# One-core hybrid decoder step: second half-batch woven by dependency strands, tanh forms, gates by tokens, value rows placed by load

## The chip, the cores and the metric

The kernel is one program on one NeuronCore of a Trainium2 chip. Its measure is device time in microseconds of that core, from launch to the last instruction. The core's engines run their own instruction streams in program order and meet only at semaphores: TensorE (PE, with its weight load PEld), VectorE (DVE), ScalarE (ACT), GpSimd (POOL) and SyncE (SP). Here POOL only issues gathers of expert rows and SP issues all other transfers.

## The reference, cut to what matters

512 prompt tokens (after 16 meta tokens) and 8 sample tokens go through one layer with D = 1024.

```python
z, xbc, dt_raw, q, k, v, g, g_lr, merge = split(rmsnorm(x) @ w_in)
xbc_c = silu(conv4(xbc)); y = ssd_chunked(...)              # 32 heads in 4 groups, chunks of 128
y_ssd = (rms((y + d_skip * xh) * silu(z)) * ssd_norm_w) @ w_ssd_out     # rms over a group of 512
o = gla_chunked(q, k, v, logsigmoid(g_lr @ up + b) / 16)    # 4 heads, chunks of 64
y_gla = (rms(o) * gla_norm_w * silu(g)) @ w_gla_out         # rms over a head's 256
x = x + (sigmoid(m0) * y_ssd + sigmoid(m1) * y_gla) @ w_out
hn = rmsnorm(x, norm2_w)
# PEER: 8 heads; top 16 of 128 x 128 keys; each chosen expert is a row (u, v) of 2 x 1024 numbers
x = x + sum_{h,k} softmax_gate * gelu(u[idx] . hn) * v[idx]
```

Everything is fp32.

## The kernel before, in words

Three stages (norm, SSD and GLA of the first 256 prompt tokens with the samples) fill the first 480 us or so. The change touches only `stage_tail`, and there it touches the planner and the task bodies.

**Two halves and a PEER loop.** The tail holds half p = 0 (256 prompt tokens and 8 samples, 264 columns: gates z and g, merge gates, output projection, second norm, queries and key scores) and half p = 1 (the other 256 prompt tokens: also SSD and GLA of these tokens, then the same). Weights come in units of 512 KB (`load`, `wring`, a ring of `WR = 4`), one unit feeding 16 PE instructions of 256 columns or 8 of 512. Half 1 has 128 units: 24 of the SSD projection (`su`), 16 of GLA (`gu`), 24 of z and g (`zu`), 40 of merge (`mg`, `my`, `mo`), 8 of output (`ou`), 16 of queries (`qu`).

**PEER units and pairs.** `UNITS` are 33 blocks of 16 expert slots: five rounds `ROUNDS` (token tiles 0, 1, the samples, tiles 2, 3); a tile has 8 units, one for each head, the samples have one. A unit has 8 pairs, 264 pairs in all. A slot is one gather (`ga`, L1684) of 128 rows of 8 KB into a ring of `RING = 10` buffers; `dot` (L2117, DVE) multiplies the u half with hn and sums, `gelu` (L1874, ACT), `gg` (L2124, DVE) multiplies with the gate, then the v half is added either on PE (`diag` L1887 on ACT, then `sum` L2467, four PE instructions of 512 columns into the ACC banks) or on DVE (`acc`, L2136). That last step frees the buffer, and POOL then issues the gather that takes its place. `ch` parts 0 to 3 (DVE) choose the experts of unit u + 2. The split between PE and DVE is fixed: in rounds 0 and 1, from the second head on, slots 0, 2, 3, 4, 6, 8, 10, 11, 12, 14 of 16 go to DVE, all others to PE.

**The order.** `tail_order` writes one list of tasks; each engine executes its own tasks of that list in that order. `peer_order` gives for each pair: dot (both slots), gelu, then `sum` and the new gathers of the pair before, choice, a stretch of half-1 work (`front` 0), gg, diag, acc of this pair, another stretch (`front` 1). The half-1 work is one fixed sequence (`ssd_second`, `gla_second`, `front_half`), cut into stretches by PE cost so that the key scores of half 1 for the second head are done at pair 120 and the rest by pair 160. A wait of one task in that sequence holds all later tasks of its engine, the PEER tasks among them.

**Half 1's gates.** z and g are computed by channels; each slab of y is transposed (`tr`), multiplied by the gate (`mul`), squared (`sq`), summed by `ss` (a PE column of ones), rooted, spread again by `bc` (PE) and applied by `scale` (DVE). silu and sigmoid are ACT functions (L1720, L1792, L1824), each of which loads an ACT table when gelu was the last function, and gelu loads its own back. The GLA state is a chain of four `go` (PE) and `gst` (DVE) steps for each head.

At the end of a round `wfl` loads norm_f over hn_cur, `fadd`, `fsq`, `fms`, `frt`, `fin` finish the tile on DVE and ACT, and SP stores it (`st`), waits for that store (`xl`) and loads the next tile.

Of the kernel before, what the change touches and what calls it, by code (L numbers as in the profile page):

```python
# [997 lines left out]
VECTOR_SLOTS = (0, 2, 3, 4, 6, 8, 10, 11, 12, 14)  # L998
VECTOR_UNITS = [u for u, (r, h) in enumerate(UNITS) if r < 2 and h >= 1]
SLOT_ENGINE = ["vector" if u in VECTOR_UNITS and s in VECTOR_SLOTS else "tensor" for u in range(len(UNITS)) for s in range(TOPK)]  # L1000
SLOT_TURN = [SLOT_ENGINE[:n].count(SLOT_ENGINE[n]) for n in range(len(SLOT_ENGINE))]
# [22 lines left out]
def ssd_second(units, put, use):  # L1024

    def project(g, r, u):
        units.add(("su", g, r, u), False)
        use("su", g, r, u)

    def convolve(g, r):  # L1030
        for kind in ("cvt", "tap", "slu"):
            for j in (2 * r, 2 * r + 1):
                put(0, kind, g, j)

    put(0, "stl", 0)
    for r in range(3):
        project(0, r, 0)
        project(0, r, 1)
        convolve(0, r)
    for g in range(GROUPS):  # L1040
        ahead = [(r, u) for r in range(3) for u in range(2)] if g + 1 < GROUPS else []

        def next_unit():
            if ahead:
                r, u = ahead.pop(0)
                project(g + 1, r, u)
                return [r] if u else []
            return []

        if g + 1 < GROUPS:  # L1050
            put(0, "stl", g + 1)
        for c in range(2):
            put(1.0, "xt", g, c)
            put(.5, "bt", g, c)
            put(1.25, "seg", g, c, 0)
            put(1.25, "seg", g, c, 1)
            put(0, "btc", g, c)
            put(0, "xd", g, c)
            for half in range(2):
                put(0, "dec", g, c, half)  # L1060
                put(0, "mxm", g, c, half)
            done = next_unit()
            put(.9, "yo", g, c)
            put(.9, "cs", g, c)
            put(0, "yof", g, c)
            for r in done:
                convolve(g + 1, r)
            done = next_unit()
            put(2.0, "yd", g, c)
            put(0, "upd", g, c)  # L1070
            put(0, "ys", g, c)
# [7 lines left out]
def gla_second(units, put, use):

    def project(h, u):
        units.add(("gu", h, u), False)
        use("gu", h, u)

    put(0, "gz")
    put(3.4, "glr")
    put(0, "glc")
    for h in range(2):
        put(0, "gsl", h)
    project(0, 0)  # L1090
    put(1.7, "gkp")
    for kind in ("gkb", "gke", "gkn", "gkd"):
        put(0, kind)
    for u in range(1, 4):
        project(0, u)
    for h in range(GH):
        nxt = lambda u: project(h + 1, u) if h + 1 < GH else None
        put(0, "qkv", h)
        put(.5, "cum", h)
        for kind in ("bnd", "gex", "qke"):  # L1100
            put(0, kind, h)
        put(1.0, "kta", h)
        put(0, "ktc", h)
        put(0, "atm", h)
        for j in range(4):
            put(1.1, "go", h, j)
            nxt(j)
            put(0, "gst", h, j)
            if j % 2:
                put(0, "goc", h, j // 2)  # L1110
        put(0, "gss", h)
        if h + 2 < GH:
            put(0, "gsl", h + 2)
        if h % 2:
            put(0, "gos", h // 2)


def front_half(p, units, seq):

    put = lambda cost, *task: seq.append((cost, task))  # L1120
    cost_of = {"zu": 3.6, "mg": 3.6, "my": 3.6, "mo": 3.6, "ou": 3.5, "qu": 3.6, "su": 3.5, "gu": 3.5}
    use = lambda *task: put(cost_of[task[0]], *task)

    put(0, "xload", p)
    if p == 1:
        ssd_second(units, put, use)
        gla_second(units, put, use)
    for s in range(6):
        for u in range(4):
            units.add(("zu", p, s, u), p == 0)  # L1130
    for j in range(KD):
        for i in range(2):
            units.add(("mg", p, j, i), p == 0)
        for u in range(2):
            units.add(("my", p, j, u), False)
        units.add(("mo", p, j), False)
# [7 lines left out]
    if p == 0:  # L1144
        put(0, "ysload", 0)
    put(0, "yload", p, 1)
    for q in range(4 if p == 0 else 0):
        put(0, "xcast", q)
        put(0, "xsub", q)
    for s in range(7):  # L1150
        t = s - 1
        for u in range(4):
            if s < 6:
                use("zu", p, s, u)
            elif u < 2:
                use("mg", p, 0, u)
            else:
                use("my", p, 0, u - 2)
            if t < 0:
                continue  # L1160
            if u >= 1:
                put(.2, "ss", p, t, u - 1)
            if s < 6 and u == 3:
                for a in range(3):
                    put(0, "silu", p, s, a)
            put(.7, "tr", p, t, u)
            for kind in (("mul", "sq") if t < 4 else ("sq", "mul")):
# [1475 lines left out]
```

## Time and profile before

| what | value |
|---|---|
| median of 3 runs | 2611.31 us (2610.52 to 3598.17) |
| profiled execution, its own time | 2614.99 us |
| its span, first to last instruction | 2612.9 us |
| PE / DVE / ACT / POOL busy over the span | 82% / 60% / 28% / 27% |
| mean granted PE clock | 0.904 of full |
| DMA | 751.20 MB, of which the expert rows (queue q0) 545.29 MB |
| first dot starts, last dot ends | 852.3 us, 2598.1 us |

The span is read in three parts: up to the first dot at 852 us (the first stages and half 0); from there to 1905 us, in which units 0 to 15 of PEER are woven with nearly all of half 1; and the rest, units 16 to 32, with the last query units in it. The highest of the three times lies far from the two others and from the profiled one; the median is the figure to compare with.

### The profile page before, as it was taken

What the parts mean: (1) busy time and instruction counts of PE and PEld (TensorE: products, weight loads), DVE (VectorE), ACT (ScalarE), POOL (GpSimd) and SP (SyncE); (2) the same over time, 40 slices, a digit from 0 to 9 for tenths busy, and PEclk for the clock granted to TensorE, in tenths of its full rate; (3) what the DMA queues carried; (4) which work ended last, traced back from release to release, by engine and by line L of the source; (5) the groups of instructions that cost most, each with busy time, mean ns of one, the idle gap of its engine ahead of it and who ended that gap; (6) DMA issues with size and microseconds to landing.
All of it is one profiled execution on the core that took longest, in us unless ns stands there. A gap on an engine that the chain in (4) does not pass through costs nothing.

```text
span 2612.9 us, 24483 instructions
## 1 busy us (share of the span) xinstructions
PE 2130.9 (82%) x7972; PEld 1348.2 (52%) x7988; DVE 1577.6 (60%) x3578; ACT 739.6 (28%) x1761; POOL 702.5 (27%) x636
## 2 busy tenths in 40 slices
PE   5888798699996967776788888997779877787786
PEld 5655365488964645553565666773525433333332
DVE  2556323233213539896666577887866777777764
ACT  2333111232102225443322333222223222222221
POOL 0212122000000222221233232333324444444452
PEclk8999799798998988888898998998879999989899
DMA  5143222442544978886788897999989999999997
GB/s 206 78 157 147 89 99 77 158 146 87 159 157 148 392 281 302 300 301 221 290 312 342 326 388 289 422 424 425 407 243 414 427 427 427 427 427 427 427 426 296
DMA packets 146402, 751.20 MB, mean 288 GB/s; under 512 B 20025, under 2 KB 39033, under 8 KB 77538
## 3 DMA queue, kind: packets, MB, share of 16 engines
q0 software_dynamic: 75008, 545.29, 52.3%
q1 hardware_dynamic: 71266, 204.33, 21.7%
q8 instruction: 64, 1.05, 0.2%
q14 instruction: 64, 0.52, 0.1%
HBM read 718.43 MB, written 31.07 MB: 287 GB/s over the span
## 4 chain that ended last, share of the span: by engine, by line
PE 41%; DVE 18%; DMA 14%; issue 4%; ACT 4%; POOL 1%; SPq 0%; DVEq 0%; POOLq 0%; ACTq 0%
PE bank L2467 12%; DMA t_rows<-in_experts,t_idx 12%; PE bank L2174 10%; PE bank L2404 6%; DVE t_rows L2117 6%; PE bank L2416 3%; DVE t_fin L2136 2%; PE bank L2176 2%; PE bank L2177 2%; PE bank L2178 2%; POOL t_rows L1684 1%; DMA t_hn_cur<-in_norm_f 1%; PE bank L2372 1%; DVE t_junk L1940 1%; DVE t_junk L1936 1%
## 5 line engine op out<-in xcount | busy, mean ns | idle before, releaser
L1684 POOL DMA_INDIRECT t_rows<-in_experts,t_idx x528 | 616.0, 1167 | 1511.9 <-PE bank L2467 662.9
L2467 PE MATMUL bank<-t_rows,t_diag 128*128 128x512 f32 (+1 forms) x1552 | 769.4, 642 | 194.6 <-ACT t_diag L1887 194.2
L2117 DVE CUSTOM_DVE_ANT_0 t_rows<-t_rows,t_hn_cur 128x1024 f32<-128x1024 f32 (+1 forms) x528 | 634.1, 1223 | 167.6 <-DMA t_rows<-in_experts,t_idx 167.3
L2467 PEld LDWEIGHTS bank<-t_rows,t_diag 128*128 128x128 f32 (+1 forms) x1552 | 296.7, 200 | 594.9 <-issue 335.8
L2174 PE MATMUL bank<-t_xs,t_wring 128*128 128x256 f32 (+1 forms) x1664 | 408.9, 403 | 46.6 <-ACT t_last L1712 23.2
L2174 PEld LDWEIGHTS bank<-t_xs,t_wring 128*128 128x128 f32 x1664 | 332.7, 203 | 133.3 <-issue 80.1
L1874 ACT ACTIVATE t_gel<-t_hid 128x2 f32<-128x2 f32 (+1 forms) x264 | 53.7, 203 | 638.2 <-DVE t_hid L2117 638.0
L1887 ACT ACTIVATE t_diag<-ident,t_gg 128x128 f32<-128x128 f32 x372 | 133.5, 395 | 189.5 <-DVE t_gg L2124 188.9
L2136 DVE SCALAR_TENSOR_TENSOR t_fin<-t_rows,t_gg,t_fin 128x1024 f32<-128x1024 f32 x140 | 179.9, 1285 | 7.8
L2404 PE MATMUL bank<-t_yoT,t_wring 128*128 128x264 f32 (+1 forms) x768 | 175.2, 386 | 4.2 <-DVE t_yoT L2076 4.2
L2404 PEld LDWEIGHTS bank<-t_yoT,t_wring 128*128 128x128 f32 x768 | 146.3, 192 | 34.2 <-issue 12.7
L1874 ACT ACT_TABLE_LOAD x78 | 100.1, 1283 | 73.4 <-DVE t_hid L2117 72.3
L2176 PE MATMUL bank<-t_xhl,t_whl 128*128 128x264 f32 x320 | 97.2, 304 | 23.5 <-DVE t_xhl L1962 22.9
L1958 DVE TENSOR_TENSOR t_whl<-t_wring,t_whl 128x1024 fp32r<-128x1024 f32 x40 | 48.9, 1223 | 78.8 <-ACT t_whl L1696 78.8
L418 PE MATMUL bank<-xnT,ring 128*128 128x280 f32 x368 | 94.4, 418 | 1.5 <-PEq L2487 1.5
L2177 PE MATMUL bank<-t_xhl,t_whl 128*128 128x264 f32 x320 | 93.3, 292 | 0.0
L2178 PE MATMUL bank<-t_xhl,t_whl 128*128 128x264 f32 x320 | 93.3, 291 | 0.0
L2124 DVE TENSOR_TENSOR t_gg<-t_gel,t_gates 128x2 f32<-128x2 f32 (+1 forms) x264 | 40.9, 155 | 81.4 <-ACT t_gel L1874 79.6
L418 PEld LDWEIGHTS bank<-xnT,ring 128*128 128x128 f32 x368 | 72.9, 200 | 20.4 <-issue 2.2
L2416 PE MATMUL bank<-t_wring,t_mixed 128*128 128x512 f32 (+1 forms) x160 | 73.6, 610 | 7.5 <-issue 7.5
L2057 DVE TENSOR_TENSOR t_yoT<-bank,t_mixed 128x264 f32<-128x264 f32 (+1 forms) x48 | 20.5, 428 | 94.2 <-PE bank L2354 39.3
L2176 PEld LDWEIGHTS bank<-t_xhl,t_whl 128*128 128x128 f32 x320 | 62.8, 196 | 24.9 <-issue 24.2
(388 smaller groups left out, 2436.0 us busy)
## 6 DMA issues: line engine op xcount, KB each, us to landing
t_wring<-in_w_merge SPq DMA_DIRECT2D x80, 512.0 KB, 4.8
t_wring<-in_w_z SPq DMA_DIRECT2D x32, 512.0 KB, 5.8
t_wring<-in_w_query SPq DMA_DIRECT2D x32, 512.0 KB, 7.9
ring<-in_w_ssd SPq DMA_DIRECT2D x4, 3072.0 KB, 13.2
t_wring<-in_w_ssd SPq DMA_DIRECT2D x24, 512.0 KB, 6.5
t_rows<-in_experts,t_idx POOLq DMA_INDIRECT x528, 14.3
s_sst<-in_state_ssd SPq DMA_DIRECT2D x4, 2048.0 KB, 9.3
o_sssd<-s_sst SPq DMA_DIRECT2D x16, 512.0 KB, 2.6
```

Of the source, the lines that this page charges most:

```text
L418: last = nc.tensor.matmul(ps[MAIN[n % 3]][:, 0:ACOLS], w[:, kt, i * P:(i + 1) * P], k.xnT[:, kt, 0:ACOLS], start=kt == 0, stop=kt == KD - 1)
L1684: nc.gpsimd.indirect_dma_start(rows[0:m, n % RING, :], None, k.dram["experts"], bass.IndirectOffsetOnAxis(idx[0:m, u, s:s + 1], 0)).then_i ...
L1874: nc.scalar.activation(gel[0:m, 2 * g:2 * g + 2], hid[0:m, 2 * g:2 * g + 2], ACT.Gelu).then_inc(gelu_done, 1)
L2117: last = nc.vector.tensor_tensor_reduce(out=v, in0=v, in1=hn_cur[0:m, r % 2, :], scale=1.0, scalar=0.0, op0=ALU.mult, op1=ALU.add, accum_o ...
L2136: nc.vector.scalar_tensor_tensor(fin[:, :], rows[:, n % RING, D:ROW], gg[:, s:s + 1], fin[:, :], ALU.mult, ALU.add).then_inc(acc_done, 1)
L2174: return nc.tensor.matmul(out, wring[:, n % WR, cols], x[:, kt, 0:w], start=first, stop=final)
L2176: nc.tensor.matmul(out, hi, xhl[:, 0, kt, 0:w], start=first, stop=False)
L2177: nc.tensor.matmul(out, lo, xhl[:, 0, kt, 0:w], start=False, stop=False)
L2178: return nc.tensor.matmul(out, hi, xhl[:, 1, kt, 0:w], start=False, stop=final)
L2404: last = nc.tensor.matmul(ps[bank][:, 0:width(p)], wring[:, n % WR, kt * P:(kt + 1) * P], yoT[:, at_k + kt, 0:width(p)], start=kt == 0 and ...
L2416: last = nc.tensor.matmul(ps[2 + 3 * i + c][0:part_rows(c), :], mixT[:, kt, part_cols(c)], wring[:, n % WR, kk * 512:(kk + 1) * 512], star ...
L2467: last = nc.tensor.matmul(ps[bank][0:round_rows(r), :], diag[0:m, d % DIAGS, 0:round_rows(r)], rows[0:m, n % RING, D + half * 512:D + half ...
```

## The change

1. **Strands.** The fixed sequence of half 1 is replaced by some 45 strands, each a list of steps with the tasks that they must follow. A "place" is half a pair (`front` 0 or 1). At each place every strand is asked in turn for steps whose predecessors were emitted at least 1 place before (2 for a step that begins on PE); PE cost is paced so that half 1 ends at place 228 (pair 114), and no place takes more than about 6 us of it. Half 0's rest is taken in gulps of 5 us a place.
2. **Pair order.** dot is one task per slot; gg, diag and acc of the pair before stand between the two dots, `sum` of the pair before follows on PE, then the place, the choice, the second place.
3. **tanh forms.** silu and sigmoid of half 1 (sigmoid of half 0 as well) become ACT Tanh and a DVE `scalar_tensor_tensor`; conv weights are halved once, and the output projection's result is multiplied by .5.
4. **Gates by tokens.** z and g of half 1 are computed by tokens (`zt`), gated and squared there, and one PE product with a diagonal of reciprocal roots (`dg`, `tq`) transposes and scales at once; `ss`, `bc`, `rc`, `scale` go for half 1.
5. **GLA.** Its units are split into `gq` and `gv`; the four chunk products come first (`csp`), one DVE task forms the four states, one PE task the outputs.
6. **Rows by load.** `slot_engines` puts each slot on PE or DVE, whichever has less planned work at that pair.

```diff
-VECTOR_SLOTS = (0, 2, 3, 4, 6, 8, 10, 11, 12, 14)
-VECTOR_UNITS = [u for u, (r, h) in enumerate(UNITS) if r < 2 and h >= 1]
...
+    strand(*[step([("sil", g, CT - 1), of("ups", prev(chunks, i))], 1.5, ("xt", g, c), ("bt", g, c)) for i, (g, c) in enumerate(chunks)])
+    strand(*[step([("bt", g, c), of("yd", prev(chunks, i)), of("mxm", prev(chunks, i), 1)], 0, ("btc", g, c), ("xd", g, c)) for i, (g, c) in enumerate(chunks)])
+    strand(*[step([of("upd", prev(chunks, i)) or ("gkd",), of("dec", prev(chunks, i), 1)], 2.5, ("seg", g, c, 0), ("seg", g, c, 1)) for i, (g, c) in enumerate(chunks)])
+    strand(*[step([("seg", g, c, 1), of("yd", prev(chunks, i))], 0, ("dec", g, c, 0), ("dec", g, c, 1)) for i, (g, c) in enumerate(chunks)])
+    strand(*[step([("xd", g, c), of("ups", prev(chunks, i)), ("stl", g)], 1.8, ("yo", g, c), ("cs", g, c)) for i, (g, c) in enumerate(chunks)])
+    strand(*[step([("dec", g, c, 1), ("btc", g, c)], 0, ("mxm", g, c, 0), ("mxm", g, c, 1)) for g, c in chunks])
+    strand(*[step([("mxm", g, c, 1), ("xd", g, c), of("upd", prev(chunks, i))], 2., ("yd", g, c)) for i, (g, c) in enumerate(chunks)])
+    strand(*[step([("yd", g, c), ("yof", g, c)], 0, ("upd", g, c), ("ys", g, c), *([("sts", g)] if c else [])) for g, c in chunks])
...
     for u in range(len(UNITS)):
         for g in range(PAIRS):
-            order.append(("dot", u, g))
+            order.append(("dot", u, g, 0))
+            if prev is not None:
+                weigh_pair(*prev)
+            order.append(("dot", u, g, 1))
             order.append(("gelu", u, g))
             if prev is not None:
                 finish_pair(*prev)
+            order.append(("front", u, g, 0))
             if g in parts and u + 2 < len(UNITS):
                 choice_part(u + 2, parts[g])
-            order.append(("front", u, g, 0))
-            order.append(("gg", u, g))
-            order.append(("diag", u, g))
-            order.append(("acc", u, g))
             order.append(("front", u, g, 1))
...
+TENSOR_LAG, OTHER_LAG = 2, 1
+PLACE_COST = 6.
+LAST_PLACE = 2 * 114
+ROW_COST = {"tensor": 1.94, "vector": 1.29}
+PAIR_TIME = 5.5
+    def run_place(goal):
+        place += 1
+        if at < len(front):
+            taken = 0.
+            while at < len(front) and taken < 5.:
+                taken += take()
+            return
+        for i, steps in enumerate(strands):
+            while heads_at[i] < len(steps):
+                after, cost, tasks = steps[heads_at[i]]
+                lag = TENSOR_LAG if tasks[0][0] in TENSOR_KINDS else OTHER_LAG
+                if any(t not in place_of or place_of[t] + lag > place for t in after):
+                    break
+                if cost and (spent + cost / 2 > goal or here and here + cost > PLACE_COST):
+                    break
...
+def slot_engines(tensor_load, vector_load):
+                late["tensor"] = max(0., late["tensor"] - PAIR_TIME) + tensor_load.get(pair, 0.)
+                late["vector"] = max(0., late["vector"] - PAIR_TIME) + vector_load.get(pair, 0.)
+                pick = "tensor" if late["tensor"] + ROW_COST["tensor"] <= late["vector"] + ROW_COST["vector"] else "vector"
...
+            if kind in ("gq", "gv"):
+                i = 256 * (kind == "gv")
+                return k.dram["w"]["gla"][p].rearrange("p (k c) -> p k c", k=KD)[:, 4 * at[0]:4 * at[0] + 4, i:i + 256]
...
-                    nc.scalar.activation(xc[:, g % 2, j, :], cv[:, j % 2, :], ACT.Silu).then_inc(slu_done, 1)
+                    nc.scalar.activation(raw[:, j % 2, HIST:HIST + BT], cv[:, j % 2, :], ACT.Tanh).then_inc(slu_done, 1)
+                elif kind == "sil":
+                    nc.vector.scalar_tensor_tensor(xc[:, g % 2, j, :], raw[:, j % 2, HIST:HIST + BT], 1.0, cv[:, j % 2, :], ALU.add, ALU.mult).then_inc(sil_done, 1)
...
+                elif kind == "gt":
+                    k.vlink(dve, nc.vector.scalar_tensor_tensor(gz[:, c, :], gz[:, c, :], 1.0, z[:, :], ALU.add, ALU.mult))
+                    nc.vector.scalar_tensor_tensor(yc[:, s % 2, c, :], gz[:, c, :], .5, yc[:, s % 2, c, :], ALU.mult, ALU.mult).then_inc(gt_done, 1)
+                elif kind == "tq":
+                    for a in range(4):
+                        for c in range(2):
+                            last = nc.tensor.matmul(ps[6 + a // 2][:, a % 2 * BT + c * P:a % 2 * BT + (c + 1) * P], yc[:, s % 2, c, a * P:(a + 1) * P],
+                                                    dg[:, c, 0 if s < 4 else a // 2, :], start=True, stop=True)
```

## Rows read from the trace of the kernel before

**Rows 1.** Busy us (and count) by engine in eight stretches; PE clock, DMA share, GB/s.
```profile
852.00:909.00 57.00, 53.37 (x205) 35.99 (x206) 29.38 (x81) 14.51 (x42) 11.98 (x12) 0.92 1.00 402
909.00:1008.00 99.00, 70.42 (x266) 49.16 (x266) 53.75 (x115) 31.80 (x75) 23.32 (x20) 0.86 0.77 275
1008.00:1223.00 215.00, 156.24 (x656) 113.78 (x661) 194.05 (x397) 99.89 (x235) 58.14 (x48) 0.87 0.82 294
1223.00:1400.00 177.00, 145.20 (x497) 96.38 (x498) 114.00 (x256) 49.25 (x115) 50.33 (x39) 0.85 0.77 286
1400.00:1600.00 200.00, 167.98 (x677) 122.77 (x675) 124.41 (x296) 70.17 (x142) 57.19 (x47) 0.90 0.90 348
1600.00:1780.00 180.00, 166.70 (x677) 128.81 (x678) 152.69 (x337) 51.20 (x99) 61.97 (x54) 0.97 0.98 401
1780.00:1905.00 125.00, 93.23 (x285) 54.96 (x284) 100.40 (x214) 29.46 (x64) 42.29 (x36) 0.85 1.02 396
...
1999.00:2597.00 598.00, 479.40 (x1049) 201.84 (x1048) 423.96 (x1110) 152.32 (x424) 268.17 (x234) 0.94 1.00 422
```
**Rows 2.** Groups by line, 852 to 1905 us: count, busy us, mean ns, idle before.
```profile
L2174 PE MATMUL bank<-t_xs,t_wring 128*128 128x256 f32 (+1 forms) x1440 | 354.5, 403 | 46.1 <-ACT t_last L1712 23.2 <-issue 15.8 <-DMA t_wring<-in_w_z 4.7
L1684 POOL DMA_INDIRECT t_rows<-in_experts,t_idx x256 | 305.8, 1195 | 745.2 <-DVE t_fin L2136 354.7 <-PE bank L2467 338.5 <-issue 52.0
L2117 DVE CUSTOM_DVE_ANT_0 t_rows<-t_rows,t_hn_cur 128x1024 f32<-128x1024 f32 x256 | 303.4, 1219 | 18.2 <-DMA t_rows<-in_experts,t_idx 18.0
...
L2467 PE MATMUL bank<-t_rows,t_diag 128*128 128x512 f32 x461 | 241.5, 656 | 59.3 <-ACT t_diag L1887 59.3
L2136 DVE SCALAR_TENSOR_TENSOR t_fin<-t_rows,t_gg,t_fin 128x1024 f32<-128x1024 f32 x140 | 179.9, 1285 | 7.8
...
L1874 ACT ACT_TABLE_LOAD x59 | 75.7, 1283 | 73.1 <-DVE t_hid L2117 72.3
...
L1967 DVE SCALAR_TENSOR_TENSOR t_mixed<-t_mixed,t_cw 128x256 f32<-128x256 f32 x72 | 33.9, 484 | 41.7 <-ACT t_mixed L1713 39.7
...
L2124 DVE TENSOR_TENSOR t_gg<-t_gel,t_gates 128x2 f32<-128x2 f32 x128 | 19.7, 154 | 56.8 <-ACT t_gel L1874 56.1
...
L2372 PE MATMUL bank<-ones,t_sq 128*128 128x1 f32 x96 | 14.0, 249 | 13.7 <-ACT t_sq L1804 13.4 <-ACT t_rs L1816 0.3
...
L1982 DVE TENSOR_TENSOR t_yoT<-bank,dte 128x512 f32<-128x512 f32 x8 | 5.5, 685 | 0.1
```
**Rows 3.** The chain that ended last, in order of time: start us, us, what.
```profile
934.18 15.78 issue
...
1394.23 16.56 DMA t_wring<-in_w_z
...
1468.87 3.54 PE bank L2467 x8
```
**Rows 4.** Groups by line, 1905 to 1999.4 us.
```profile
L2117 DVE CUSTOM_DVE_ANT_0 t_rows<-t_rows,t_hn_cur 64x1024 f32<-64x1024 f32 (+1 forms) x32 | 38.3, 1218 | 5.7 <-DMA t_rows<-in_experts,t_idx 5.7
...
L2174 PE MATMUL bank<-t_xs,t_wring 128*128 128x256 f32 x64 | 16.0, 406 | 0.0
```
**Rows 5.** Groups by line, 1999.4 us to the end.
```profile
L2117 DVE CUSTOM_DVE_ANT_0 t_rows<-t_rows,t_hn_cur 128x1024 f32<-128x1024 f32 x240 | 292.4, 1227 | 143.8 <-DMA t_rows<-in_experts,t_idx 143.6
...
L2174 PE MATMUL bank<-t_xs,t_wring 128*128 128x256 f32 x64 | 14.5, 379 | 0.0
```
**Rows 6.** Timeline at 1001 us: start us, us, engine line and operation.
```profile
1001.50 0.40 ACT L1887 ACTIVATE t_diag<-ident,t_gg 128x128 f32<-128x128 f32 x1 [1.34 <-DVE t_gg L2124]
...
1001.96 3.26 PE L2467 MATMUL bank<-t_rows,t_diag 128*128 128x512 f32 x4 [0.47 <-ACT t_diag L1887]
```
**Rows 7.** DMA issues, 1600 to 1905 us: count, KB each, median us to landing.
```profile
t_wring<-in_w_merge SPq DMA_DIRECT2D x32, 512.0 KB, 8.2
...
t_rows<-in_experts,t_idx POOLq DMA_INDIRECT x90, 19.3
```
**Rows 8.** DMA issues, 1008 to 1223 us.
```profile
t_rows<-in_experts,t_idx POOLq DMA_INDIRECT x48, 8.0
```

More of the change, by code:

```diff
@@ L1079, in gla_second @@
[L1079 to L1115, printed above, removed]
@@ new lines, with emit @@
+TENSOR_LAG, OTHER_LAG = 2, 1
+PLACE_COST = 6.
+LAST_PLACE = 2 * 114
+VECTOR_COST = {"tap": 1.45, "sil": .5, "xd": 2.05, "mxm": .7, "yof": 2.1, "ups": .7, "upd": .7, "qke": 1.3, "atm": .45, "gst": 1.95, "gt": 1.4,
+               "dg": 1., "mix": 1.3, "x1": .7, "hn": 1.6, "hms": .2, "bnd": .15, "gkd": 1.4, "gz": 1., "fadd": 1.4, "fin": 1.6, "dot": 1.3, "gg": .16}
+CHOICE_COST = (2., 2., 2.6, 2.4)
+ROW_COST = {"tensor": 1.94, "vector": 1.29}
+PAIR_TIME = 5.5
+def tail_order(units):
+    front = with_loads(units, first_half(units))
+    first = len(units.names)
+    strands = second_half()
+    count = first + sum(t[0] in UNIT_KINDS for steps in strands for _, _, tasks in steps for t in tasks)
+    total = sum(cost for steps in strands for _, cost, _ in steps)
+    peer = peer_order()
+    order, at, place, spent, places = [], 0, 0, 0., 0
+    emitted, place_of = set(), {}
+    heads_at = [0] * len(strands)
+    tensor_load, vector_load, pair = {}, {}, 0
+    def emit(task, cost=0.):
+        order.append(task)
+        emitted.add(task)
+        place_of[task] = place
+        tensor_load[pair] = tensor_load.get(pair, 0.) + cost
+        vector_load[pair] = vector_load.get(pair, 0.) + (CHOICE_COST[task[2]] if task[0] == "ch" else VECTOR_COST.get(task[0], 0.))
+        if task[0] in UNIT_KINDS and task not in first_names:
+            units.add(task, False)
+        if task[0] in UNIT_KINDS or task[0] == "zu":
+            n = number[task] if task in first_names else len(units.names) - 1
+            if n + WR < count and n + WR >= first:
+                order.append(("load", n + WR))
+    first_names = set(units.names)
+    number = {name: n for n, name in enumerate(units.names)}
@@ L1326, in until @@
     def until(task):
+        stuck = 0
         while task not in emitted:
-            take()
-    until(("sc", 0, 1))
-    cost = sum(c for c, t in front[at:])
-    late = [i for i, (c, t) in enumerate(front) if t == ("sc", 1, 1)][0]
-    early_cost = sum(c for c, t in front[at:late + 1])
-    rest_cost = cost - early_cost
-    pairs_early, pairs_late = 8 * 15, 8 * 5
-    pair = 0
-    base = 0.
+            if at < len(front):
+                take()
+            else:
+                before = len(order)
+                run_place(1e9)
+                stuck = 0 if len(order) > before else stuck + 1
+                assert stuck < 50, (task, [steps[i] for steps, i in zip(strands, heads_at) if i < len(steps)])
@@ L1344, in tail_order @@
         if kind == "front":
[L1345 to L1357 removed]
+            places += 1
+            pair = places // 2
+            if start is None and at >= len(front):
+                start = places
+            goal = 0. if start is None else total * (places - start + 1) / (LAST_PLACE - start)
+            run_place(goal)
             continue
```

771 lines of the change are left out of this document (461 added, 310 removed).

## The prediction

> **What bounds the kernel now.** I read the stretches first (busy time of each engine, clock and DMA share), then the groups by line inside the worst of them, then the chain. The reader is to see two regimes. From about 2000 us DMA is the bound: share 1.00 at 422 GB/s [rows 1], and the dots wait 143.6 us for rows [rows 5]; a pair of rows takes 598/120 = 4.98 us there. Between 852 and 1905 us it is not: 256 dots [rows 2], which are units 0 to 15, take 1053 us, 8.2 us a pair. Dots wait only 18 us for rows there, while POOL waits 355 us for a DVE row sum and 339 us for a PE one before it may refill a buffer [rows 2]. So the ring is emptied too slowly: the woven work bounds it. Inside that span the bound changes. In 1008 to 1223 (SSD) DVE is busy 194 of 215 us. In 1223 to 1400 (GLA) nothing is full: PE 145 of 177, DVE 114, DMA share 0.77. In 1600 to 1780 (merge) PE is busy 167 of 180 at clock 0.97 and DMA is at 0.98: there the weave works [rows 1]. Two whole stalls stand in the chain: PE's 15.78 us from 934 (half 1's activations are loaded only after half 0's last query) and 16.56 us for a late weight [rows 3].
>
> **The sum** has three terms: to the first dot; the woven stretch W, in which the changed kernel does 114 pairs with all of half 1; and the rest.
>
> **First term.** Half 0 keeps its planner sequence; its sigmoid becomes tanh, with the same count of ACT and DVE instructions. I price it at nothing; if a table had to be loaded twice in each of the eight merge steps and nothing hid it, 16 x 1.283 us [rows 2] = 21 us. 852 us stay.
>
> **Last term.** 264 - 114 = 150 pairs. The old trace runs units 16 to 32 from 1905 to the end, 708 us; eight query units are in it (128 instructions of 16 a unit [rows 4, 5]), 8 x 0.524 MB at 422 GB/s = 10 us of DMA, which move into W. Fourteen more pairs (units 14.25 to 15) at 4.98 us add 70. Sum 768 us. The new pair order frees a buffer one dot of the next pair later, about 2.5 us of the ring's turn of 10 x 2.49 = 25 us. That costs nothing as long as the other transfers stay in flight: rows land in 19.3 us where DMA is full [rows 7] but in 8.0 us where it is not [rows 8], so ten to eleven of the nineteen are queueing. Uncovered it would be 2.5 us in each of 30 turns, 75 us; I keep that for the range.
>
> **W by engine.** PE is busy 853 us in the seven stretches to 1905 [rows 1]. Removed: the sums `ss`, 14.0 us [rows 2]; `tr` becomes `tq`, 48 instructions for 48. Rows: now 461/4 = 115 on PE. The planner's own numbers give some 571 us of PE cost over 110 pairs, 5.2 a pair, and on DVE 2.6 for dots, 0.16, 1.1 for the choice and 1.5 for half 1, 5.4. Its balance 5.2 + 1.94k = 5.4 + 1.29(2 - k) gives k = 0.86 PE rows a pair, 98 in 114 pairs: 17 fewer at 3.54/2 = 1.77 [rows 3], -30 us. Added: the eight query units, 16.0 + 14.5 = 30 us [rows 4, 5]. PE's need is 840 us at the mean clock of these stretches (0.89, weighted by length), or 770 at the merge stretch's 0.97. In the merge stretch PE reaches a busy share of 167/180 = 0.93 [rows 1]; if strands bring that everywhere, W is 770/0.93 = 830 to 840/0.93 = 905. I take the middle, 870, because fuller PE will keep more, not all, of the clock.
>
> DVE: 769 us now [rows 1]; 28 dots fewer (-34), 10 row sums fewer at 1.285 (-13), 24 `sil` at 0.484 (+12) and 24 `gt` of 512 columns at 0.685 (+16), less about 10 for `mul` and `scale` of like shape [rows 2]: 740. At the SSD stretch's share of 0.90 that is 820, under PE's. DMA: 228 rows of 1.049 MB, 139 units (128, and 11 queries of half 0) of 0.524 MB, some 15 MB of states, y and keys: 327 MB at 422 GB/s = 775 us. PE is the bound, the others close under it. GLA's units become rows of 1 KB; 16 loads, like the `su` loads, land in time with a ring of four, priced at nothing. POOL and SP add no instructions of weight.
>
> The 15.78 us stall stays (the same load, the same release): W = 870 + 16 = 886. Total 852 + 886 + 768 = 2506 us of span, and 2 us lie around it (2614.99 against 2612.9): 2508 us, **2510** rounded. The profiled execution lies 4 us above the median, so this is 101 us, 3.9%, under the median.
>
> **Where the gain comes from.** The strands put one or two places between a task and what it needs, so a late ACT or DVE step no longer stops the dots behind it; gg gets a dot's cover for gelu, whose wait was 56.1 us [rows 2]. The tanh forms: gelu's own table loads are 59 in W, 1.283 us each [rows 2], beside like loads for the function that displaced it. No tanh is in this trace, so whether it lives with gelu isn't shown: if not, the loads stay; if so, some 26 pairs of loads go, 67 us of an ACT that is busy 28%. Bounds: 0 to the 56 us of the gg wait, which the new order covers anyway; I take 0. The Trainium skill, "ScalarE: Activation LUTs", section on table sets, lists gelu as a set of its own and tanh with exp and with sigmoid; by it every tanh would still displace gelu's table and the sum would stay as it is. The row of 1.283 us agrees with that page's load time; which set serves tanh here no row shows.
>
> **Rivals.**
> A. *The new pair order closes a loop (no gain).* `sum` of a pair now needs gg, which stands on DVE behind the first dot of the next pair and behind the DVE tasks of the second place; where such a task needs PE's first place of the same pair (lag 1), one pair is one turn: DVE task 3 x 0.685, dot 1.22, gg 0.15, diag 0.40 and the hop of 0.06 [rows 2, 6] with two more like it, `sum` 1.5 (k = 0.86), PE place 2.5: 8.1 us; with both rows on PE, as in SSD where DVE is full, 10.2. All queued on PE behind `sum` (the weave) and on POOL (gathers) waits with it. If 37 SSD pairs turn at 10.2 and 73 at 8.1, and the first four pairs and the stall take 76, W = 1045 and the time 2665. Against it: without the loop a pair costs (886 - 76)/110 = 7.4, and by the strands an SSD chunk (7 places) has three such edges, half of them in the second place: 0.43 a pair, 0.25 over all. It costs the 2% from a third of the pairs on, and all the gain from two thirds on.
> B. *SP holds back weights.* At a round's end SP waits in order for the store before it loads further units, and several new SP waits (`gsl`, `yload`, `gss`) stand between loads. One such stall was 16.56 us [rows 3]; five would be 83: 2590. Against it: a weight lands in 8.2 us with DMA full [rows 7], under three units of 3.5.
> C. *DMA becomes the bound throughout.* W = 775 + 16: about 2410 to 2450. For it: the merge stretch does just that; against it: PE's need at any clock seen is about as large.
> D. *The strands don't spread the work.* The chains (SSD 7 places a chunk, GLA 9 a head, then one merge unit a place) leave light and heavy stretches; the sum of the largest demand stage by stage, at 7.9 us a pair in SSD, 6.9 in GLA, 8.2 in z, 7.7 in merge, 7.0 after it, gives W near 919 and 2540: still the forecast's side. If pairs stay at 8.2 and more, 2570.
>
> **Chances and range.** Forecast with D's first form (2450 to 2558) 0.60; C 0.10; A 0.17, of it 0.10 within 2%; B 0.10; D's last form 0.03. 2% is 52 us (2559 to 2664), about what a measurement of this kernel can tell from no change. Faster 0.60 + 0.10 - 0.02 for its edge = 0.68; same 0.10 + 0.10 + 0.03 + 0.01 = 0.24; slower 0.07 + 0.01 for a tail that keeps the 75 us = 0.08. The range leaves out half of C and most of A: 2430 to 2615. The likeliest case alone is 2450 to 2558.
>
> **What would show it.** Right: 228 dots of the woven stretch in about 886 us; PE's busy share over 0.9 with a clock near 0.93 in SSD and GLA; the dots' wait for rows grows; half 1's last query near pair 114; 4.98 us a pair after it. Rival A shows as PE waiting before L2467 on `diag` with DVE waiting for PE in the same stretch; B as PE waiting for wring; C as a share near 1 from 910 us on. I am wrong if SSD pairs still take 9 us, if pairs after the weave take more than 5.1 us, or if ACT is the one waited for.

## The result, and the profile after

| what | before | after |
|---|---|---|
| median of 13 runs each | 2613.99 us | 2600.54 us |
| ratio, 95% interval | 1 | 0.9949 (0.9937 to 0.9962) |
| profiled execution, its span | 2614.99, 2612.9 us | 2599.58, 2597.4 us |
| PE / DVE / ACT / POOL busy | 82 / 60 / 28 / 27% | 82 / 61 / 26 / 26% |
| mean granted PE clock | 0.904 | 0.911 |
| first dot; pair 114; pair 128; unit 18 | 852.3; 1808.6; 1905.4; 1999.5 us | 847.4; 1790.1; 1869.4; 1974.8 us |

The change brings 0.5%, where 3.9% was forecast. The highest run of each kernel (3598.17 and 11567.10 us) lies far from all others, and the medians hardly feel it. The last line of the table takes the starts of the dots from the traces; with the span it gives the lengths that return in every experiment: W (first dot to pair 114), the pairs from there to unit 16 (which begins with pair 128), units 16 and 17, and unit 18 to the end.

Stretches of the kernel after: bounds, us; busy us (and count) of PE, PEld, DVE, ACT, POOL; PE clock, DMA share, GB/s.

```profile
847.00:1790.00 943.00, 793.61 (x2940) 530.90 (x2948) 710.03 (x1555) 276.05 (x699) 273.47 (x227) 0.91 0.90 346
...
1790.00:1870.00 80.00, 62.04 (x200) 36.04 (x200) 62.97 (x151) 20.26 (x54) 30.92 (x29) 0.96 1.02 393
1885.00:1940.00 55.00, 54.56 (x64) 8.36 (x64) 27.07 (x76) 9.91 (x29) 17.33 (x15) 0.50 0.84 255
1975.00:2580.00 605.00, 461.73 (x959) 182.83 (x957) 416.05 (x1110) 149.73 (x417) 248.88 (x234) 0.95 1.00 416
```

In W (the first row) nothing is full: PE is busy 794 of 943 us, a share of 0.84, DVE 0.75, DMA 0.90. In the last row DMA is the bound, as in [rows 1], but at 416 GB/s and not 422.

What PE waited for in W (us in total, times, longest us), first of the kernel before, then of the kernel after:

```profile
PE bank L2467 <- ACT t_diag L1887: 37.2, 9, 12.5
PE bank L2174 <- ACT t_last L1712: 23.2, 8, 6.1
PE bank L2223 <- ACT t_yoT L1720: 18.8, 4, 4.7
PE bank L2174 <- issue: 15.8, 1, 15.8
PE bank L2317 <- DVE t_yoT L2034: 15.2, 4, 4.1
PE bank L2372 <- ACT t_sq L1804: 13.4, 6, 5.7
```
```profile
PE bank L2671 <- ACT t_diag L2016: 100.7, 34, 12.6
PE bank L2341 <- issue: 17.2, 1, 17.2
PE bank L2656 <- ACT t_q L1981: 9.7, 2, 8.9
PE bank L2341 <- ACT t_last L1799: 5.6, 1, 5.6
PE bank L2424 <- DVE t_rs L2159: 5.5, 1, 5.5
```

Two things are to be seen. The waits of half 1's own chain shown here (`t_last`, `t_yoT`, `t_sq` before; `t_q`, `t_last`, `t_rs` after) fall from 71 us to some 20. That is what the strands are built for, but no run here has the strands alone, and `t_sq`'s wait goes because `ss` goes. And one wait has grown from 37 to 101 us: the sums of a pair (L2671) for their diagonals. The x-load stall (`issue`) stays, as predicted.

One turn of that wait, from the timeline at 1232 us (start us, us, engine line and operation, and in brackets the idle time before it with what ended it; lines between are left out):

```profile
1233.64 0.16 DVE L2291 TENSOR_TENSOR t_gg<-t_gel,t_gates 128x2 f32<-128x2 f32 x1
...
1233.83 0.69 ACT L2016 ACTIVATE t_diag<-ident,t_gg 128x128 f32<-128x128 f32 x2 [4.08 <-DVE t_gg L2291]
1234.28 5.71 PE L2671 MATMUL bank<-t_rows,t_diag 128*128 128x512 f32 x8 [5.39 <-ACT t_diag L2016]
...
1239.83 3.62 PE L2487 MATMUL bank<-t_wring,t_xs 128*128 128x256 f32 x16
1243.28 1.90 PE L2449 MATMUL bank<-t_yoT 128*128 128x64 f32 x16
1245.01 3.67 PE L2487 MATMUL bank<-t_wring,t_xs 128*128 128x256 f32 x16
1245.21 0.69 DVE L2147 TENSOR_TENSOR t_mixed<-t_mixed,bank 128x512 f32<-128x512 f32 x1 [7.84 <-PE bank L2449]
1246.75 1.16 DVE L2285 CUSTOM_DVE_ANT_0 t_rows<-t_rows,t_hn_cur 128x1024 f32<-128x1024 f32 x1
...
1247.84 0.15 DVE L2291 TENSOR_TENSOR t_gg<-t_gel,t_gates 128x2 f32<-128x2 f32 x1
```

PE stands 5.39 us before the sums, then does the place that is queued behind them (L2487, L2449). DVE stands 7.84 us for that place's product, and the next pair's dot and gg are queued behind DVE's wait. Each engine waits in turn for the other: rival A of the prediction. In the 10 us before the first gg shown DVE waits for nothing; it works through the choice and half 1's tasks that stand ahead of that gg in its list. So PE waits for DVE's work, and then DVE for PE's.

### The profile page after: what moved, and what is told of

It reads as the page before. It is cut to its first block, busy times and chain, and to the rows that moved or that the text cites. A ratio compares the mean times of both kernels' runs of the same rounds, so it can differ in the third digit from the quotient of the medians.

```text
span 2597.4 us, 23895 instructions
## 1 busy us (share of the span) xinstructions
PE 2122.3 (82%) x7708; PEld 1285.6 (49%) x7724; DVE 1571.6 (61%) x3594; ACT 684.7 (26%) x1730; POOL 684.0 (26%) x636
## 4 chain that ended last, share of the span: by engine, by line
PE 39%; DMA 17%; DVE 16%; issue 5%; ACT 3%; POOL 1%; SPq 0%; DVEq 0%; ACTq 0%; POOLq 0%
DMA t_rows<-in_experts,t_idx 15%; PE bank L2671 13%; PE bank L2341 7%; PE bank L2608 6%; DVE t_rows L2285 5%; DVE t_fin L2303 2%; PE bank L2620 2%; PE bank L2343 2%; PE bank L2374 2%; PE bank L2344 2%; PE bank L2345 2%; ACT t_diag L2016 1%; PE bank L2487 1%; POOL t_rows L1770 1%; DVE t_mixed L2098 1%
## 5 line engine op out<-in xcount | busy, mean ns | idle before, releaser
L2671 PE MATMUL bank<-t_rows,t_diag 128*128 128x512 f32 (+1 forms) x1560 | 806.3, 668 | 281.8 <-ACT t_diag L2016 281.5
L1770 POOL DMA_INDIRECT t_rows<-in_experts,t_idx x528 | 598.0, 1133 | 1518.0 <-PE bank L2671 775.5
L2285 DVE CUSTOM_DVE_ANT_0 t_rows<-t_rows,t_hn_cur 128x1024 f32<-128x1024 f32 (+1 forms) x528 | 641.2, 1220 | 205.2 <-DMA t_rows<-in_experts,t_idx 203.1
L2671 PEld LDWEIGHTS bank<-t_rows,t_diag 128*128 128x128 f32 (+1 forms) x1560 | 303.8, 203 | 754.8 <-issue 388.2
L2341 PE MATMUL bank<-t_xs,t_wring 128*128 128x256 f32 (+1 forms) x1280 | 300.0, 392 | 27.7 <-issue 17.2
L2341 PEld LDWEIGHTS bank<-t_xs,t_wring 128*128 128x128 f32 x1280 | 248.5, 196 | 80.4 <-issue 42.4
L2089 DVE TENSOR_TENSOR t_whl<-t_wring,t_whl 128x1024 fp32r<-128x1024 f32 x40 | 48.9, 1223 | 78.2 <-ACT t_whl L1783 78.2
L2374 PE MATMUL bank<-t_wring,t_xs 128*128 128x512 f32 x192 | 84.7, 594 | 1.4 <-DMA t_wring<-in_w_z 0.9
L578 DVE SCALAR_TENSOR_TENSOR s_cv<-s_raw,s_cw,s_cv 128x272 f32<-128x272 f32 x72 | 40.6, 564 | 52.2 <-ACT s_cv L532 50.4
```

The source lines that it names most:

```text
L1770: nc.gpsimd.indirect_dma_start(rows[0:m, n % RING, :], None, k.dram["experts"], bass.IndirectOffsetOnAxis(idx[0:m, u, s:s + 1], 0)).then_i ...
L2285: nc.vector.tensor_tensor_reduce(out=v, in0=v, in1=hn_cur[0:m, r % 2, :], scale=1.0, scalar=0.0, op0=ALU.mult, op1=ALU.add, accum_out=hid[ ...
L2341: return nc.tensor.matmul(out, wring[:, n % WR, cols], x[:, kt, 0:w], start=first, stop=final)
L2374: last = nc.tensor.matmul(ps[2 + 2 * (s % 2) + c][:, :], xs[:, 2 * u + kk, c * P:(c + 1) * P], wring[:, n % WR, kk * 512:(kk + 1) * 512], ...
L2671: last = nc.tensor.matmul(ps[bank][0:round_rows(r), :], diag[0:m, d % DIAGS, 0:round_rows(r)], rows[0:m, n % RING, D + half * 512:D + half ...
```

## The experiments

Every ratio is against the kernel before on the same chip, with its 95% interval. The edits are to the kernel after, or to the experiment named.

| run | ratio | W, us | PE's wait on diag in W, us | pairs 114 to 128 | units 16, 17 | unit 18 to end |
|---|---|---|---|---|---|---|
| before | 1 | 956.2 | 37.2 | 96.8 | 94.1 | 613.3 |
| after | 0.9949 | 942.7 | 100.7 | 79.3 | 105.4 | 622.6 |
| e1 | 0.9834 (0.9808 to 0.9861) | 923.0 | 84.4 | 75.1 | 103.6 | 620.1 |
| e2 | 0.9750 (0.9724 to 0.9775) | 893.7 | 53.1 | 79.6 | 104.5 | 620.3 |
| e3 | 0.9701 (0.9678 to 0.9723) | 875.4 | 41.1 | 84.7 | 105.3 | 622.9 |
| e4, on before | 1.0123 (1.0101 to 1.0145) | 982.3 | 97.7 | 94.4 | 101.6 | 614.7 |
| e5 | 0.9637 (0.9597 to 0.9677) | 871.1 | 43.6 | 82.0 | 105.4 | 613.5 |
| e6 | 0.9757 (0.9715 to 0.9800) | 882.1 | 56.1 | 94.6 | 105.1 | 613.8 |
| e7 | 0.9639 (0.9598 to 0.9680) | 868.6 | 38.0 | 81.6 | 105.4 | 612.7 |
| e8 | 0.9631 (0.9590 to 0.9672) | 872.4 | 35.3 | 74.5 | 103.3 | 613.5 |
| e9 | 0.9616 (0.9571 to 0.9661) | 870.4 | 41.1 | 80.3 | 98.9 | 613.5 |
| e10 | 0.9789 (0.9747 to 0.9831) | 911.2 | 80.2 | 82.0 | 106.6 | 613.0 |
| e11 | 0.9586 (0.9546 to 0.9627) | 866.0 | 35.8 | 78.6 | 102.1 | 612.3 |
| e12 | 0.9667 (0.9628 to 0.9706) | 872.7 | 40.6 | 79.2 | 104.6 | 613.8 |

**The pair order.** Four runs take the new order apart: e1 puts gg, diag and acc ahead of both dots and so takes the dot out of the loop, e2 puts the whole old order back, e3 moves the woven place ahead of the sums, and e4 puts the new order on the kernel before, without strands.

e1:
```diff
-            order.append(("dot", u, g, 0))
             if prev is not None:
                 weigh_pair(*prev)
+            order.append(("dot", u, g, 0))
             order.append(("dot", u, g, 1))
```


> The changed kernel with gg, diag and acc of the pair before moved ahead of both dots (they stood between the dots). Theory P (the pair order closes the loop: PE waits 101 us for diag in the woven stretch because gg stands behind the next pair's first dot): each wait gets shorter by up to a dot, 1.2 us, on about 110 pairs; PE's wait for diag in the woven stretch falls to 40 to 70 us, and round ends no longer wait for the next round's rows: 2540 to 2575 us. Theory R (the coupling is by the strands' lags and by DVE's total work; the wait on diag only shows where PE is early): the wait moves elsewhere, 2590 to 2605 us.

e2:
```diff
             order.append(("dot", u, g, 0))
-            if prev is not None:
-                weigh_pair(*prev)
             order.append(("dot", u, g, 1))
             order.append(("gelu", u, g))
             if prev is not None:
                 finish_pair(*prev)
-            order.append(("front", u, g, 0))
             if g in parts and u + 2 < len(UNITS):
                 choice_part(u + 2, parts[g])
+            order.append(("front", u, g, 0))
+            weigh_pair(u, g)
             order.append(("front", u, g, 1))
...
-    weigh_pair(*prev)
```


> The changed kernel with the old pair order (dot, dot, gelu, sums of the pair before, choice, first place, gg, diag, acc of this pair, second place); strands, tanh, gates and rows by load stay. Theory P: the second place covers diag, PE's wait for it falls under 40 us in the woven stretch, but DVE may wait for gelu again (56 us in the kernel before): 2520 to 2570 us. Theory R: 2590 us or more, since strands alone bring nothing.

e3:
```diff
             order.append(("gelu", u, g))
+            order.append(("front", u, g, 0))
             if prev is not None:
                 finish_pair(*prev)
-            order.append(("front", u, g, 0))
             if g in parts and u + 2 < len(UNITS):
                 choice_part(u + 2, parts[g])
```


> The changed kernel with the first half-pair place ahead of the pair's sums, so that on PE a place's 2.5 us of work covers gg and diag. Theory P: PE's wait for diag falls to 20 to 50 us, the time to 2530 to 2570 us. Theory R: 2590 to 2610 us. Buffers come free one place later; if the ring were what binds, it would be slower than 2600 us.

e4: `peer_order` of the kernel after (a dot for each slot, gg, diag and acc between the two dots of the next pair, the sums ahead of the place) in the kernel before, with its fixed sequence and its fixed slots.

> The kernel before with the new pair order alone (dots as single tasks, gg, diag, acc of the pair before between them, sums after gelu, choice between the places). Theory P: PE's wait for diag grows above its 59 us, the pairs after the weave lose about 1%: 2630 to 2690 us. Theory R: the order does nothing by itself, 2600 to 2625 us.

W falls in step with the wait: 943 us with 101, 923 with 84, 894 with 53, 875 with 41. e3 is the sharpest of the four. Away from the ends of the rounds it changes the list of PE alone, the other engines' lists are the same, and it is worth 67 us of W, of which 41 lie in pairs 16 to 39 (SSD) and 19 in pairs 40 to 62 (GLA). DVE's waits for PE in W fall with it, from 94 us in 19 waits after to 43 us in 13 (e1 72 us, e2 58 us). The same place of the work in e3, from its timeline, again with lines left out:

```profile
1194.32 0.16 DVE L2291 TENSOR_TENSOR t_gg<-t_gel,t_gates 128x2 f32<-128x2 f32 x1
...
1194.96 5.40 PE L2671 MATMUL bank<-t_rows,t_diag 128*128 128x512 f32 x8 [1.94 <-ACT t_diag L2016]
...
1200.20 1.89 PE L2449 MATMUL bank<-t_yoT 128*128 128x64 f32 x16
1202.13 0.69 DVE L2147 TENSOR_TENSOR t_mixed<-t_mixed,bank 128x512 f32<-128x512 f32 x1 [4.07 <-PE bank L2449]
1203.67 1.16 DVE L2285 CUSTOM_DVE_ANT_0 t_rows<-t_rows,t_hn_cur 128x1024 f32<-128x1024 f32 x1
1204.75 0.16 DVE L2291 TENSOR_TENSOR t_gg<-t_gel,t_gates 128x2 f32<-128x2 f32 x1
```

One of the two L2487 groups has been done before the sums; PE's wait is 1.94 us and not 5.39, DVE's 4.07 and not 7.84, and the gg shown last comes 10.4 us after the one shown first and not 14.2. The stretch of W shows a second effect, in e3 and then in e5:

```profile
849.00:1724.00 875.00, 767.59 (x2948) 521.73 (x2948) 709.46 (x1554) 276.34 (x699) 269.96 (x227) 0.94 0.95 372
```
```profile
855.00:1726.00 871.00, 767.79 (x2948) 522.30 (x2948) 709.40 (x1555) 276.44 (x699) 270.13 (x227) 0.94 0.95 374
```

The same 2948 PE weight loads and almost the same matmul records take PE 768 us at clock 0.94, where after took 794 at 0.91. Of the 68 us between the two stretches 26 are this, and 42 are idle time of PE: the wait on diag falls by 60, other waits grow by some 18. A PE that waits less is also granted more here. e1 gains 20 us of W alone, and next to the moved place nothing (e8 against e5, below): the dot lengthens the loop but doesn't close it. e4 costs the kernel before 1.2%, with W 26 us longer and the wait on diag up from 37 to 98 us, so the loop comes with the pair order and doesn't need the strands. Two expectations were missed in part: e1 keeps 84 us of the wait where 40 to 70 were expected, and e2 53 where under 40 were.

**The ring's address.** After W, the pairs of units 18 to 32 take 5.07 us in the kernel after and 5.00 before. The ring of row buffers starts 64 bytes lower in a partition (27,584 and not 27,648), since the change's small tiles `zss` and `eps` are placed ahead of it. e5 is e3 with both behind the ring.

```diff
-        zss = sb("zss", [P, 2, 2])
-        eps = sb("eps", [P, 1])
...
         rows = sb("rows", [P, RING, ROW])
+        zss = sb("zss", [P, 2, 2])
+        eps = sb("eps", [P, 1])
```


> The run with the place before the sums, and the two new small tiles (zss, eps) allocated after the row ring instead of before it, so that the ring starts again at byte 27648 of a partition, a multiple of 512, where the kernel before has it (the changed kernel has it at 27584). Theory A (the 1.4% by which pairs after the weave are slower, 5.06 to 5.07 us against 5.00, comes from the ring's address): 5.00 us a pair, units 18 to 32 take 613 to 615 us instead of 623, whole 2525 to 2533 us. Theory S (it comes from the missing query work or from the new order): the pairs stay at 5.06 us, 2537 to 2543 us.

The time from unit 18 to the end falls from 622.9 to 613.5 us, 4.99 us a pair, which is that of before. Its stretch moves 422 GB/s where the kernel after has 416:

```profile
1915.00:2510.00 595.00, 460.65 (x958) 182.75 (x956) 415.36 (x1108) 150.08 (x416) 248.10 (x234) 0.95 1.00 422
```

All kernels with the ring at the lower address (after, e1 to e3) have 620 to 623 us there; all with it at the higher (before, e4 to e12) have 612 to 615.

**The rest of W and its end.** e6 paces half 1 to end later (`LAST_PLACE = 2 * 125`), e7 halves the gulps of half 0's rest (`taken < 2.5`), e8 puts gg, diag and acc ahead of both dots, each on e5.

> The run before this one with half 1 paced to end at pair 125 (LAST_PLACE = 2 x 125) instead of 114. If the sample round is slow (105 us for units 16 and 17 against 94 before) because PE then has only sums and its clock falls to 0.55, later queries give back 5 to 10 us there, and the woven pairs have less PE work each: 2505 to 2525 us. If the round's end itself (store, norm_f, sums of 64 rows) sets it, nothing moves there, and 114 pairs get faster only by what the later pairs lose: 2525 to 2535 us.

> The aligned run with half 0's last queries taken in places of 2.5 us instead of 5 (one unit a place, done at pair 5 instead of 2). If the gulps starve the ring at the start (units 0 and 1 take 168 us against 156 before), 5 to 15 us come back; if half 1's start sets the weave's end, it is the same or up to 10 us slower.

> The aligned run with gg, diag and acc of the pair before ahead of both dots. Theory P: with the place covering diag 41 us of PE's wait on diag are left; two dots less ahead of them should take off half, 15 to 20 us. Theory R (the rest of the wait is DVE's own lag, whatever stands ahead): within 5 us of the aligned run.

e6 is a miss: later queries were to ease the woven pairs and to give back 5 to 10 us in units 16 and 17; W grew by 11 us, pairs 114 to 128 by 13, and the two units stay at 105. As its planner ends the queries with pair 127, none stands in unit 16, so it says nothing on what query work there would do. The pace is also what `slot_engines` plans with; 111 of the first 228 rows go to PE and not 97. e7 makes no difference beyond its interval: units 0 and 1 take 154.5 us and not 165.0, but pairs 16 to 39 take 189.5 and not 177.7. e8 leaves W as it is and takes 7.5 us from the pairs behind it; in the total (0.9631 against 0.9637) that can't be told from nothing.

**Units 16 and 17.** They take 103 to 107 us in the kernels whose query units are gone from there, 94 before. e9 is e5 with eight spare bf16 products of 512 columns a pair in these two units, whose result nothing reads.

```diff
+                    if u in (16, 17):
+                        if u == 16 and g == 0:
+                            pe.wait_ge(qc_done, 2 * EH)
+                        for _ in range(8):
+                            nc.tensor.matmul(ps[4][:, :], k.identb[:, :], k.future[:, :], start=True, stop=True)
                     for s in range(2 * g, 2 * g + 2):
```


> The aligned run with the place first, in which PE issues 8 extra 512-column bf16 products into an unused bank ahead of each pair's sums in units 16 and 17 (they are not part of the computation). Theory C (units 16 and 17 take 105 us against 94 before because the query units that stood there before are gone, PE's clock falls to 0.55 and 0.69, and PE's sums then hold the ring): the clock rises above 0.8 and the two units take 90 to 97 us, the whole 8 to 15 us less than the aligned run. Theory E (the round's end itself, with its store and loads, sets them): 105 us or more, the whole the same or slower.

The sample round's sums as the chain that ended last has them (start us, us, what), first after, then e9, then before:

```profile
1868.36 14.02 DMA t_hn_cur<-in_norm_f
...
1885.44 54.78 PE bank L2671 x64
```
```profile
1804.86 13.57 DMA t_hn_cur<-in_norm_f
...
1821.49 6.98 PE bank L2676 x8
1828.47 3.53 PE bank L2665 x8
1832.00 4.13 PE bank L2676 x8
1836.14 1.83 PE bank L2665 x8
1837.97 3.53 PE bank L2676 x8
```
```profile
1920.23 6.98 PE bank L2467 x8
1927.21 4.83 PE bank L2174 x16
1932.04 3.53 PE bank L2467 x8
```

In after the 64 sum products take 0.86 us each and the granted clock of their stretch is 0.50, which is 1.2 of 2.4 GHz. In e9 and before the first eight take 0.87 us each too: all three kernels come out of the wait for the norm weights at the low clock. But in e9 PE has the spare products (L2665) between, and from the third pair on a sum product takes 0.44 us, at a clock of 0.94:

```profile
1828.00:1868.00 40.00, 40.00 (x113) 9.62 (x112) 20.22 (x58) 6.94 (x21) 14.08 (x14) 0.94 0.88 286
```

Before, query units stood there (L2174) and the clock rose as well: 104 PE instructions in 41 us, at 0.88.

```profile
1920.00:1961.00 41.00, 40.77 (x104) 13.27 (x104) 28.15 (x78) 10.71 (x32) 16.18 (x15) 0.88 0.88 283
```

The sample round's sums have a shape of their own: its tile has 64 rows for 8 tokens, and they take 64 rows by 8 columns of PE's array (64*8), as this line of e5's timeline shows:

```profile
1849.42 23.24 PE L2671 MATMUL bank<-t_rows,t_diag 64*8 64x512 f32 x27
```

The query products, the spare products and the sums of the other rounds are 128*128. In each of the three traces the granted clock rises only once such a product has run: at 1929.6 us before (L2174 from 1927.1), at 1833.2 in e9 (L2665 from 1828.5), and in after at 1951.7, when the next round's sums have begun at 1947.5. Whether it is their shape, their type or something else that counts was not tried.

e9 gives back 6.5 of the 11 us, a little less than expected (units 16 and 17 at 90 to 97 us, 98.9 measured); the total lies 0.2% under e5's, within the interval. What the other 5 us are stays open. The missing query work need not be all of the 11 us: in e4 the query units still stand there, and with the new pair order the two units take 101.6 us.

**Rows by load.** e10 is e5 with the fixed slots of before.

```diff
+                pick = "vector" if r < 2 and h >= 1 and s in (0, 2, 3, 4, 6, 8, 10, 11, 12, 14) else "tensor"
                 late[pick] += ROW_COST[pick]
```


> The aligned run with the place first, with the kernel before's fixed slots on DVE instead of rows by load: 105 of the first 228 rows on PE instead of 97, but 40 instead of 47 of the first 80 (start and SSD), 17 instead of 31 of the next 46 (GLA), 35 instead of 7 of the 66 in the z and merge stretch. If rows by load matter: PE gets 28 rows x 1.77 = 50 us more in the z and merge stretch, where it is the fullest, and loses 21 rows = 37 us before; the whole 15 to 45 us slower. If not: within 8 us of the aligned run.

W grows by 40 us and the wait on diag from 44 to 80. The number of rows on PE hardly differs (414/4 = 104 against 97); where they lie does. The total is within the 15 to 45 us expected, but not by the expected parts: the first 40 pairs, where PE has fewer rows, were to be faster and are 13 us slower, and pairs 63 to 113 are 31 us slower.

**All together, and the price of the functions.** e11 puts e3, e5, e7, e8 and e9 into one kernel. e12 is e5 with Silu and Sigmoid in place of Tanh; the DVE steps stay, so it computes other values, and only its time is read.

> The four edits that each gave something are put together: the place ahead of the sums (e3), the ring at the address of before (e5), gg, diag and acc ahead of both dots (e8), half 0's gulps at 2.5 us (e7) and eight spare products a pair in units 16 and 17 (e9), whose results nothing reads. If the gains act on different stretches they add up: W about 870 us, pairs 114 to 128 about 75 (as in e8), units 16 and 17 about 99 (as in e9), the rest 613.5; first dot at 848: 2506 us of span, a ratio near 0.959. If DMA at the end of W sets pairs 114 to 128 and the next round together, what e9 gives is taken back by e8's earlier end and the time stays at 2517 to 2520.

> e5 with the ACT function of slu and th set back to Silu and that of sig to Sigmoid; every task, wait and DVE instruction stays, so the output is another one (the second DVE step of each form is still applied). What is left is the price of the function alone. If the functions sit in another table than gelu, table loads come back: about 24 for Silu in the SSD chunks and 12 in z, 8 for Sigmoid in the merge steps of each half, each with a reload before the next gelu, at 1.28 us a load. Theory of the prediction (ACT is off the path, price 0): W stays within 10 us of e5's 871 and the time within 10 us of 2524.7. Rival (gelu is in the loop dot, gelu, gg, diag, sum, so each reload stretches one pair by up to 1.3 to 2.6 us): W longer by 20 to 60 us, time 2545 to 2585, and PE's wait on diag up from 44 us.

e11 takes 2508.68 us (median), the lowest of this study: 4.1% under the kernel before, though its interval overlaps those of e5, e7, e8 and e9. Each part, and the sum, lies within some 4 us of what was expected. e12 brings back 41 table loads in W, and ACT's busy time there rises from 276 to 329 us, which is 41 x 1.28:

```profile
L2003 ACT ACT_TABLE_LOAD x52 | 66.7, 1283 | 71.4 <-DVE t_hid L2285 70.8
...
L1804 ACT ACT_TABLE_LOAD x12 | 15.4, 1283 | 0.2
...
L1952 ACT ACT_TABLE_LOAD x8 | 10.3, 1283 | 6.8 <-PE bank L2540 3.6 <-DVE t_mixed L2253 3.1
L1886 ACT ACT_TABLE_LOAD x6 | 7.7, 1283 | 0.3 <-issue 0.2
```

These lines are of W; e5 has 37 loads there on these four lines. W stays: 872.7 against 871.1 us, and the wait on diag is 41 against 44. The rival (20 to 60 us) falls.

## Why the prediction was wrong

The measured span is 91 us above the sum. By its terms, the last one split at unit 16 (us):

| term | forecast | after | e5 | e11 |
|---|---|---|---|---|
| to the first dot | 852 | 847.4 | 855.2 | 851.0 |
| W | 886 | 942.7 | 871.1 | 866.0 |
| 14 pairs to unit 16 | 70 | 79.3 | 82.0 | 78.6 |
| units 16 to 32 | 698 | 728.0 | 718.9 | 714.4 |
| span | 2506 | 2597.4 | 2527.3 | 2510.1 |

1. **First term.** Right, within 5 us; e12, with Sigmoid in half 0, has 852.1 us, so tanh there costs nothing that shows.
2. **PE's need in W.** 770 to 840 us was worked out, 794 are measured. k = 0.86 was right too: 384 sum products are 96 rows in W, 98 were forecast. So was DMA's load: 346 GB/s over 943 us are 326 MB, 327 were forecast.
3. **The failing step: a busy share of 0.93 in all of W.** It was taken from the merge stretch of before [rows 1], where the old order stood. After has 0.84 with the x-load stall, which the sum counts apart, and 0.86 without it (794 of 926 us). What it left out is rival A, which the prediction had written down with its place (gg behind the next pair's dot on DVE, sums first on PE) and held at 0.17. It was weighed by a count: 0.43 of the pairs with an edge in SSD, 0.25 over all, and a third needed for 2%. The wait on diag occurs 34 times in 114 pairs, 0.30, so the count was near; but each is 3.0 us in the mean, up to 12.6, and PE's clock falls with it. With 0.25 to 0.43 counted against a threshold of a third, the sum still charged the loop at nothing. e3 shows the step in isolation: with the place ahead of the sums, W is 875 us, 11 under the forecast of 886. But that 875 meets the forecast is luck in part: the share is still only 0.88 (768 of 875 us; 0.90 without the stall of 23.6 us), and PE's need is 768 us at a clock of 0.94, under the 770 to 840 worked out.
4. **What closes the loop** was named rightly, but not weighed. The prediction named the dot ahead of gg and the DVE task that needs PE's place behind the sums. e1 takes the dot away and gets 20 us of W; putting the place ahead of the sums gets 67, and both together no more than the latter. The link that counts is PE's: a product that DVE waits for stands behind sums that wait for DVE.
5. **The new order costs nothing in the tail.** Right for the order: the rest has 5.07 us a pair with the new order (after) and 5.06 with the old one (e2), both at the lower address. The 9 us by which unit 18 to the end is longer than before are the ring's address (e5), which the prediction didn't look at.
6. **The 10 us for the query units that move** were booked as DMA time of units 16 to 18. They weren't to be had: around these two ends of rounds the norm weights' load and PE's sums set the pace, not DMA (share 0.84 in the sample's stretch), and without the products PE's clock stayed low after that load. So the 10 us didn't come, and 11 more were added, of which e9 gives 6.5 back.
7. **14 pairs at 4.98** take 79 us: half 1's work ends near pair 119 and not 114, and the stretch moves 393 GB/s and not 422. It moves 31.46 MB, 2.1 MB more than the rows of 14 pairs: 75 us at 422. The rest is at its end: up to 1859 us it moves 420 GB/s, in the last 11 us 227 at a DMA share of 1.04. By then the ring is being filled with the sample round's rows, 64 to a gather (issued from 1850.1 us on). The prediction priced all 14 pairs at the pace of full gathers.
8. **Tanh at 0.** The price was right (e12), the reason given for it was uncertain and is now known. From the first dot to pair 128 after has 36 gelu loads where [rows 2] has 59, and a load at L1804, L1886 or L1952 only 4 times in the whole run, for 24, 12 and 32 tanh instructions: in these programs tanh is served without displacing gelu's table. The Trainium skill, "ScalarE: Activation LUTs", section on table sets, lists gelu in a set of its own and tanh with exp and with sigmoid; by it the loads would have stayed. The measurement decides against it here. The time is the same either way (e12), with ACT busy only 276 of 943 us.
9. **Rivals B and C.** Not seen in W: the waits of PE there show the weights' ring for some 2 us, and the DMA share is 0.90. In e3 and e5 it is 0.95: with the loop open DMA is close behind PE, and a share of 1 would leave 0.95 x 871 = 827 us, an estimate. e5, e7, e8, e9 and e11 all stand at 866 to 872.

In one sentence: strands, tanh, gates by tokens and rows by load are together worth 3.6% once the pair order and the ring's address are mended (e5), and the order that came with them took 2.5 points of it back, the address 0.6. Of the parts, tanh is worth nothing in time (e12) and rows by load 1.5% (e10); strands, gates by tokens and the new GLA order were not tried apart.

## What to carry to other kernels

When two in-order engines each hold work that the other needs, look at what stands directly behind a waiting instruction on each of them: the producer that the other engine waits for must stand ahead of the wait, not behind it. A loop of this kind isn't a threshold: price it at every occurrence, and count a PE clock that falls with the share of waiting. After a change that adds small buffers, look whether the large DMA targets have moved; and when work leaves a quiet stretch, look at PE's clock there.

## What the runs showed of the hardware

- Gathers of 8 KB rows into a ring that starts 64 bytes lower in the partition ran at 416 and not 422 GB/s where DMA is the bound (5.07 and 4.99 us a pair). Which alignment matters was not tried; two addresses are compared.
- 64 fp32 products of 512 columns on 64*8 of the array, back to back with PE busy 54.6 of 55 us, were granted a clock of 0.50 throughout, after the wait for the round's norm weights (14 us). With eight spare bf16 products on 128*128 a pair among them the clock was 0.94 after the first pairs, and before, with query products on 128*128 among them, 0.88.
- Gathers of 64 rows of 8 KB moved 208 GB/s (1860 to 1870 us of after), gathers of 128 rows 423 GB/s (1840 to 1850 us), at a DMA share of 1.0 in both.
- 41 more table loads, 53 us of ACT, cost no time that could be measured.
